# Four side slots for conditioning rows: ten chunks in the mixer seam, ten between the layers

## What is computed

```python
m = (silu(c) @ cond_w + cond_b).reshape(c.shape[0], 9, 1, D_MODEL)   # D_MODEL = 1024

def pre(i, h):
    return rmsnorm(h, norm_pre[i]) * (1.0 + m[:, 3 * i + 1]) + m[:, 3 * i]

def post(i, h, y, rw):
    return h + rw * m[:, 3 * i + 2] * rmsnorm(y, norm_post[i])

x = post(0, x, swiglu(pre(0, x), ffn_w_in[0], ffn_w_out[0]), 0.5)
x = post(1, x, mixer(pre(1, x)), 1.0)
x = post(2, x, swiglu(pre(2, x), ffn_w_in[1], ffn_w_out[1]), 0.5)
```

## Time and profile before

| | us |
|---|---|
| median of 3 runs | 1402.75 |
| lowest, highest | 1401.98, 1404.49 |
| the profiled execution | 1407.09 |
| its span, first to last instruction | 1405.1 |
| PE busy in it | 1340.8 |
| DVE busy | 810.6 |
| ACT busy | 587.0 |
| POOL busy | 50.5 |

### The profile page before, as it was taken

How to read it: one execution, slowest core, us unless ns; L and a number is a source line. 1 busy time by engine, 2 the same in 40 slices (tenths; PEclk the granted TensorE clock), 3 DMA queues, 4 the chain that set the end, 5 groups by cost and what they waited for, 6 DMA issues and landing times.

```text
span 1405.1 us, 34485 instructions
## 1 busy us (share of the span) xinstructions
PE 1340.8 (95%) x13990; PEld 1277.4 (91%) x13990; DVE 810.6 (58%) x1200; ACT 587.0 (42%) x965; POOL 50.5 (4%) x131
## 2 busy tenths in 40 slices
PE   6999999899989899999989999998998998999997
PEld 4999999899976899999989999998997787999997
DVE  2554453567894655554475555446789657555444
ACT  2533333543564643333463333345236555333442
POOL 4000000100020000000000000001001000000000
PEclk9999999999999999999999999999999998999998
DMA  9978789689989895577588557976997993565552
GB/s 331 273 231 253 209 272 294 185 259 325 293 275 324 251 308 150 157 218 208 164 259 253 150 160 225 318 202 208 324 327 223 319 324 94 152 177 152 145 163 84
DMA packets 423816, 324.49 MB, mean 231 GB/s; under 512 B 15559, under 2 KB 351719, under 8 KB 423696
## 3 DMA queue, kind: packets, MB, share of 16 engines
q1 hardware_dynamic: 421124, 317.03, 74.2%
q0 software_dynamic: 2272, 5.61, 1.3%
q10 hardware_dynamic: 300, 0.13, 0.0%
HBM read 317.93 MB, written 4.78 MB: 230 GB/s over the span
## 4 chain that ended last, share of the span: by engine, by line
PE 83%; DVE 6%; DMA 3%; SPq 3%; ACT 2%; DVEq 1%; issue 1%; ACTq 0%
PE PS L573 23%; PE PS L574 22%; PE PS L575 22%; PE PS L597 4%; PE PS L618 2%; PE PS L825 1%; PE PS L619 1%; PE PS L620 1%; SPq L466 1%; PE PS L871 1%; DMA direct<-in_cache_sb_v 1%; DVE w_lo L1610 1%; DMA raw<-in_ffn_w_in 1%; SPq L445 1%; ACT Y L1288 1%
## 5 line engine op out<-in xcount | busy, mean ns | idle before, releaser
L1610 DVE TENSOR_TENSOR w_lo<-raw,w_hi 128x1024 fp32r<-128x1024 f32 (+1 forms) x368 | 392.6, 1106 | 458.9 <-ACT w_hi L1230 458.7
L1230 ACT ACTIVATE w_hi<-raw 128x1024 fp32r<-128x1024 f32 (+1 forms) x368 | 336.9, 960 | 674.5 <-PE PS L575 601.6
L573 PE MATMUL PS<-a_hi,w_hi 128*128 128x288 f32 x1760 | 524.5, 298 | 0.6 <-issue 0.6
L574 PE MATMUL PS<-a_lo,w_hi 128*128 128x288 f32 x1760 | 519.7, 295 | 0.0
L575 PE MATMUL PS<-a_hi,w_lo 128*128 128x288 f32 x1760 | 518.1, 294 | 0.0
L573 PEld LDWEIGHTS PS<-a_hi,w_hi 128*128 128x128 f32 x1760 | 330.1, 188 | 3.8 <-issue 3.5
L575 PEld LDWEIGHTS PS<-a_hi,w_lo 128*128 128x128 f32 x1760 | 331.6, 188 | 0.0
L574 PEld LDWEIGHTS PS<-a_lo,w_hi 128*128 128x128 f32 x1760 | 330.6, 188 | 0.9 <-issue 0.7
L574 PE MATMUL PS<-h_lo,w_hi 128*128 128x288 f32 x704 | 209.1, 297 | 0.0
L573 PE MATMUL PS<-h_hi,w_hi 128*128 128x288 f32 x704 | 208.7, 296 | 0.0
L575 PE MATMUL PS<-h_hi,w_lo 128*128 128x288 f32 x704 | 208.5, 296 | 0.0
(11 more groups left out here) (320 smaller groups left out, 1119.8 us busy)
## 6 DMA issues: line engine op xcount, KB each, us to landing
raw<-in_ffn_w_in SPq DMA_DIRECT2D x176, 512.0 KB, 5.1
direct<-in_cond_w SPq DMA_DIRECT2D x288, 256.0 KB, 5.2
direct<-in_cache_sb_k SPq DMA_DIRECT2D x128, 256.0 KB, 4.3
direct<-in_cache_sb_v SPq DMA_DIRECT2D x128, 256.0 KB, 4.3
raw<-in_ffn_w_out SPq DMA_DIRECT2D x64, 384.0 KB, 3.7
raw<-in_mix_w_in SPq DMA_DIRECT2D x48, 512.0 KB, 7.3
raw<-in_ffn_w_out SPq DMA_DIRECT2D x64, 320.0 KB, 4.3
raw<-in_mix_w_out SPq DMA_DIRECT2D x16, 512.0 KB, 7.7
```

The costliest lines, as they stand in the source:

```text
L573: pe.matmul(out, whi, hi, start=begins and i == 0, stop=False)
L574: pe.matmul(out, whi, lo, start=False, stop=False)
L1230: act.activation(w_hi[:, s, at_:at_ + n], raw[:, s, at_:at_ + n], ACT.Copy)\
L1610: tt(w_lo[:, s, at_:at_ + n], raw[:, s, at_:at_ + n], w_hi[:, s, at_:at_ + n], ALU.subtract).then_inc(lo_done.sem, 1)
```

## The change

Four tiles of 8 KB per partition, `side0` to `side3`, take four more chunks (slots of 1 MB). `side0` and `side1` lie in the memory of `a_hi` and `a_lo`, which is idle during the output products. `side2` and `side3` lie where the mixer has `lrw_hi`, `lrw_lo`, `lr_raw` and some of what follows them. They serve group 2 of each layer and group 1 of layer 1. Twelve chunks of such a group are now eight in `direct` and four in `side`.

- **PE.** Behind the output chunks of the first FFN only two chunks are left of six (behind output chunk 5). `mixer_seam` has ten. `layer_seam` has ten in place of seven, and the input products of layer 1 two in place of five. The sums of squares of `x` are made pair by pair (`pair_squares`), with a chunk between them.
- **PSUM.** The sums of the three column blocks `c` go to three neighbouring ranges of banks 6 and 7, so that PE need not wait for a copy between them. `copy_wide` takes three at once.
- **SP.** The order of the loads of the rows: four for `direct`, two into `side2` and `side3`, for the first FFN two more for `direct`, and two into `side0` and `side1`, all between the loads of output weights.
- **POOL** waits for the fourth `side` chunk, where it waited for the sums of squares of `y`.
- **ACT** waits for the second `side` chunk before it writes `a_hi`.
- Two semaphores for the spread roots become one (`root_spread`).

```diff
+            def part_chunk(l, i, c, slot):
+                k = direct_in[slot]
+                pe.wait_ge(k.sem, (k.at(l, DP_C[i] // 4 + 1) + c // 2) * 64)
+                if c == 0 and slot % 2 == 0:
+                    pe.wait_ge(cond_copied.sem, cond_copied.at(l, 6 * i - 6))
+                cond_products(direct[:, slot, :], slot, c).then_inc(direct_used.sem, 1)
+
+            def side_chunk(l, i, slot):
+                pe.wait_ge(side_in.sem, side_in.at(l, i - 1) * 64 * NSIDE)
+                cond_products(side[slot][:, :], slot, 1).then_inc(side_used.sem, 1)
...
-                        if s % 3 == 2 and not final:
+                        if s == 2 and n == 0:
+                            for slot in (2, 3):
+                                part_chunk(l, 1, 2, slot)
+                        elif s % 3 == 2 and n == 1 and not final:
                             for c in ((7, 8, 9), (10, 11))[s // 3]:
                                 cond_chunk(l, *cond_in, *divmod(c, 4))
...
-                group(0, True, 4 if n == 0 else 0)
+                group(0, True)
                 if n == 0:
                     group(1, chunks=2)
...
-                filled_seam(l, 0, 1, DP_C[2], 6, 10, 12, l)
+                mixer_seam(l)
...
-                    filled_seam(l, 2, 0, DP_C[1], 0, 4, 7, l + 1)
+                    layer_seam(l)
```

The parts on SP, ACT, DVE and POOL:

```diff
-                        if i * 4 + s < 10:
-                            cond(l, 2, i, s)
+                        if i == 0:
+                            cond_part(lc, x, 0, s)
+                        if i == 1 and s >= 2:
+                            if l + n and s == 2:
+                                sp.wait_ge(ss_out.sem, ss_out.at(l + n, 0) * 32)
+                            cond_side(lc, x, s)
+                        if i == 2 and s < 2 and n == 0:
+                            cond_part(lc, x, 2, s)
+                        if i == 2 and s >= 2:
+                            sp.wait_ge(w_used.sem, w_used.at(l, POS_IN[n] + N_IN))
+                            cond_side(lc, x, s - 2)
...
+                if p < 2:
+                    act.wait_ge(side_used.sem, side_used.at(l, NSIDE * p - NSIDE + 2))
...
+            def copy_wide(l, i):
+                for pair in range(2):
+                    dve.wait_ge(direct_used.sem, direct_used.at(l, DP_C[i] + 4 + 2 * pair + 2))
+                    cp(crow[:, :].rearrange("p (c h x) -> p c h x", h=2, x=P)[:, :, pair, :],
+                       PS[:, 6 + pair, 0:3 * P].rearrange("p (c x) -> p c x", x=P))
+                dve.drain()
+                dve.sem_inc(cond_copied.sem, 6)
...
-                for pair in range(2):
-                    copy_sums(direct_used.at(l, DP_C[2]), 2, pair)
+                copy_wide(l, 2)
...
-                after(ssy_done, l, 1)
+                after(side_used, l, NSIDE)
```

More of the change, by code:

```diff
@@ L232, in decoder_step @@
         assert at[0] <= TOP, at[0] - TOP
+        side = [tile(f"side{j}", [P, 2048], F32, here) for j, here in enumerate(
+            (a_region, a_region + 8192, crow_end, crow_end + 8192))]
+        assert a_region + 16384 <= a_end
         dm = tile("dm", [P, GP, T], F32, y_region)
@@ L526, in _ @@
                 mix_in(0, 1)
-                cond_seam(l, 2, 10, 12)
+                for s in range(2, 4):
+                    cond_part(l, 2, 2, s)
                 mix_in(2, 3)
@@ L552, in _ @@
                         ffn_in(l + 1, 0, s, s)
-                    cond_seam(l + 1, 1, 4, 8)
+                    for s in range(4):
+                        cond_part(l + 1, 1, 2, s)
             for h in range(2):
@@ L753, in filled_seam @@
                     cond_chunk(layer, x, dp, *divmod(n, 4))
-                seam_squares(l, seam)
+                for j in range(KP):
+                    pair_squares(l, seam, j)
                 spread_x(*divmod(3 * l + seam + 1, 3))
@@ L1760, in ffn @@
                         hidden(j, j % 2)
-                        if j % 3 == 2 and not final:
+                        if j == 2 and n == 0:
+                            copy_wide(l, 1)
+                        elif j % 3 == 2 and n == 1 and not final:
                             for c, pair in (((1, 1), (2, 0)), ((2, 1),))[j // 3]:
```

133 lines of the change are left out of this document (83 added, 50 removed).

## The result

| | before | after |
|---|---|---|
| median, us | 1404.13 (6 runs, 1401.98 to 1405.47) | 1391.54 (6 runs, 1389.11 to 1392.85) |
| profiled execution | 1407.09 | 1392.76 |
| its span | 1405.1 | 1391.0 |
| mean granted clock | 0.973 | 0.981 |

The ratio is 0.9911, with a 95% interval of 0.9898 to 0.9924: 12.6 us less.

A forecast was written before the change was run, and what follows sets the result against it. PE, busy 95% of the span, was taken as the bound, with unused PE time in the seams. Terms 8.3 + 3.0 + 0.5 + 0.4 = 12.2 us, off the median 1402.75, gave 1390.5 us, range 1388.7 to 1396.0.

The forecast's parts named there:

- Output products, 8.3: Output products of the first FFN: two pairs of chunks leave in each layer, 2.08 us a pair, 8.3 us gained.
- Input products of layer 1 and first step between the layers, 3.0 + 0.4: Layer 1's input products go from five chunks to two, 3.0 us; between the layers the first step ends 0.4 us earlier.
- The seam takes the chunks up: Seam before the mixer: six chunks between the spreads, three more than before, leave `spread_x` as early or a tenth or two later.
- the tight fit: Seam before the mixer: six chunks and three sums take 7.04 us by printed durations, in a room of 6.99 us.
- The clock, 0.5: Mixer seams: the clock stays at 2.4 GHz, `spread_x` takes 0.46 us and not 0.72, 0.26 us gained in each, 0.5 us.
- a rival of chance: The clock falls all the same in the seams: 8.7 us gained, 1394.0 us, up to 1400; chance 0.22.
- Layer 0's first mixer step, taken as 0, bounds 0 to 1.3: Layer 0's mixer: the first step ends 1.6 us earlier, but later waits may take it back; gain 0 to 1.3, taken as 0.
- The load that was to hold the last chunk up: Behind `spread_x` in layer 0's mixer seam: the last chunk's load arrives at 284.33 both before and after, so it sets that chunk.
- `copy_wide`, 1.0 for two, and POOL: Mixer: two wide copies take 1.0 us (0.5 to 1.4); POOL's last small load lands at 287.9, 6.9 us after issue.
- the wait of 0 to 0.4: Mixer, each layer: PE, ready at 291.8, waits up to 0.4 us for `copy_wide` ending at 292.2; counted as 0.
- 0.7 us to spare: Layer 0's mixer: POOL's last small load lands at 287.9, 0.7 us before ACT wants it, so nothing is late.
- The sum: Whole kernel: 8.3 + 3.0 + 0.5 + 0.4 = 12.2 us, set against the median 1402.75, gives 1390.5 us.

The follow-up runs named there:

- light loads: Changed kernel, but SP's row loads inside the two new kinds of seam carry 32 of 512 columns, so the conditioning is stale: 1390.47 us in one execution.
- the run with one chunk more: Changed kernel with one idle chunk (16 products nobody reads) added between the two spreads of each new seam, ahead of the first sum: 1397.34 us, 0.9951.
- the run with the third seam interleaved: Changed kernel with chunks also put between the sums of squares of x before the second FFN, three in both layers: 1395.06 us, 0.9941.
- the run with the sums last: Changed kernel with the sums of squares of x behind all chunks between the spreads in the new seams, as before the change: 1392.52 us, 0.9919.
- the second run: The changed kernel once more, unchanged, beside the last experiment: 1391.58 us, 0.9914.
- the run with POOL 6.8 us later: Changed kernel with POOL's small loads and clearing held back until the first pair of the mixer's operands is ready: 1390.07 us, 0.9902.
- Idle products for warmth: Idle chunks between sums: in the changed kernel before the second FFN, 1391.16 us, 0.9907; in the kernel before, mixer and layer seams, 1408.07 us, 1.0027.

## Why the prediction was right, and where not

- **Output products, 8.3.** Exact: 4.16 in each layer, and 2.08 a pair when one was put back. This is the mechanism of the prediction, and it is shown both ways.
- **Input products of layer 1 and first step between the layers, 3.0 + 0.4.** Came as 2.86. The 3.0 is right: from the last product of the first step on, the stage takes 126.76 us before and 123.79 after, 2.97 less. The 0.4 was the step that failed. The last product of the first step starts 21.55 us behind the sums of `y` before and 21.66 after. The prediction let `spread_x` and DVE's operands come as before and the three chunks run through. The chunks stopped for 1.10 us, but that is the small part: with light loads and no stop the last product starts at 21.54. The larger part is that `spread_x` comes 10.69 us behind the sums of `y` and not 10.42, and the third pair of operands 18.32 and not 18.00. The delay starts on ACT, ahead of `spread_y`:

```profile
708.89 0.26 ACT L1368 ACTIVATE rstd<-rstd 128x72 f32<-128x72 f32 x1 [0.37 <-issue]
```

  This pause is 0.37 us in all ten profiles with the changed program, and 0.07 before (from the end of the one at 714.81 to 715.21). What ACT waits for there no run shows.
- **The seam takes the chunks up.** Right: in layer 0 10.48 us from the sums of `y` to `spread_x` before and after, in layer 1 10.63 and 10.48. But it was not the tight fit that was counted. From start to start the six chunks leave room for a seventh, as the run with one chunk more shows. What is tight is something the prediction didn't know: where the borders of PE's instruction blocks fall. That the long stops of the mixer seams stand behind `spread_x`, where the first step absorbs them, and not ahead of it, is luck.
- **The clock, 0.5.** It held in the three filled seams in both profiles of the changed kernel. It is not certain: it fell in the run with the third seam interleaved, at the same code, behind a stop of 0.31 us, and in the run with the sums last. The prediction called that a rival of chance without a run that showed it; now there is one. Its price was set too high, as the run with the sums last shows. The Trainium skill, "TensorE: Matmul & The Clock Gate", "What's actually happening", on which the prediction drew for this rival, says that the number of slow matmuls differs from run to run of one kernel. The trace agrees: the two profiles of the changed kernel have a mean granted clock of 0.981 and 0.989.
- **Layer 0's first mixer step, taken as 0, bounds 0 to 1.3.** This was mis-sized. The stage gained 1.16 us in layer 0, 0.9 more than the clock's 0.26, and it was not given back: the mixer's end stands 5.46 us earlier, the turn 5.38. The argument was that the loads hold a faster PE up, as in layer 1, where PE idled 1.4 us. But PE is never idle in 288 to 366, and the 1.4 us were not all a wait for loads. They are two rows of before, and the third is all that is idle in layer 1 after:

```profile
1006.36 0.86 PE L825 MATMUL PS<-direct,qb 128*32 128x128 f32 x24 [0.84 <-DVE direct L1877]
1020.82 0.29 PE L573 MATMUL PS<-a_hi,w_hi 128*128 128x288 f32 x1 [0.56 <-issue]
...
1007.83 0.29 PE L604 MATMUL PS<-a_hi,w_hi 128*128 128x288 f32 x1 [1.26 <-issue]
```

  0.56 of the 1.4 is a stop for instructions, 1.43 us behind the end of a block. The time of the step itself was worked out well: its end at 291.8, less the 4.22 by which the sums of `y` start earlier, is 287.58, and the last product starts at 287.63. The load that was to hold the last chunk up didn't: in the second run, which has no stop there, the first step starts 14.48 us behind the sums of `y`, where 14.75 was counted. In layer 1 the same stage took 0.15 more. DVE pauses there in all ten profiles with the changed program, so that the second pair of operands comes 2.16 us behind the first and not 1.89:

```profile
954.17 0.88 DVE L1806 SCALAR_TENSOR_TENSOR a_lo<-Y,M,a_hi 128x256 fp32r<-128x256 f32 x2 [0.18 <-issue]
```

  Of the 0.35 us that the first pair gains (14.68 to 14.33 behind the sums of `y`) the third keeps 0.07. And the turn has to wait for `copy_wide`, which ends at 959.55 + 1.02 = 960.57, and the turn starts at 960.65; before the change the copies ended at 973.73 and the turn began at 974.13.
- **`copy_wide`, 1.0 for two, and POOL.** Two wide copies take 1.01 us:

```profile
286.88 1.01 DVE L1710 COPY crow<-PS 128x384 f32<-128x384 f32 x2
...
274.90 1.03 POOL L2310 DMA_DIRECT2D lr_raw<-in_mix_w_in  x1 [249.93 <-PE PS L632]
...
sb_col<-in_sb_bias POOLq DMA_DIRECT2D x1, 0.0 KB, 5.0
```

  They end at 287.89, right ahead of the turn at 287.98, so the wait of 0 to 0.4 is there: PE's last product starts at 287.63, and 0.13 later it would be free. POOL began 0.8 us behind the fourth `side` chunk, as counted. The landing took 5.0 us and not the 6.9 of the earlier trace rows, and ACT did not wait. 0.7 us to spare was on the careful side, as the run with POOL 6.8 us later shows: there the DMA engines moved 16 GB/s from 281.6 to 288.5, and a landing takes 2.2 to 3.0 us, where they moved 231 from 274.9 to 282.0 in after.
- **The sum.** Forecast 12.2; the four changed stages gave 12.2, of parts that missed by -0.5, +0.9 and -0.4. That the sum agrees to a tenth is luck; that the chunks which left the full stretches gave 8.32 and 2.97, forecast with 8.3 and 3.0, is not. The measured 12.6 holds these and whatever the unchanged stages add or take in one pair of executions.

**Open:** what ACT and DVE wait for in their pauses of 0.37 and 0.18 us; whether the block of instructions starts late because of the DMA traffic, of which one run speaks; and what decides, at the same code, whether the clock falls.

## What to carry to other kernels

Price a move from start to start in a stretch where the engine is never idle, and look for its new place in a stage where a chain of other engines sets the end: 8.3 and 3.0 us came as 8.32 and 2.97. The effects on the clock were small or chance. Count the gap from start to start as well, since printed durations overlap and make it look full. And when an engine stops with no releaser, look at the landings of its instruction blocks. One chunk more did not overfill the gap, but moved such a stop ahead of the chain that sets the end, and cost three times its own duration. Idle products for warmth gained at most 1.5 us in the one stage where nothing else needed PE, and nothing for the kernel.

## What the runs showed of the hardware

- PE can run out of instructions: it stops inside a run of short independent products with no semaphore, for up to 2.35 us, and goes on 1.25 to 1.53 us after a 16 KB block of the instruction queue has landed. The places lie at fixed counts of products, 128 apart, the length differs from run to run. Long products are not exempt: 288.0 to 366.0 has no stop (78.00 us of 78.00, at 333 GB/s), but in layer 1 PE stops behind product 10373, inside products of 128x288, for 0.22 to 1.26 us in eight profiles (1007.83 in after).
- The granted clock fell at the same code at which it held. In the changed kernel it held with this ahead, and with the third seam interleaved it fell at 280.3 with the second line ahead:

```profile
276.50:279.90 3.40, 2.12 (x61) 1.77 (x65) 2.16 (x5) 2.54 (x7) 3.40 (x5) 1.00 1.07 281
```

```profile
276.90:280.30 3.40, 2.04 (x60) 1.29 (x53) 2.27 (x5) 2.56 (x6) 3.40 (x6) 1.00 1.02 303
```

- A small load from POOL lands in 4.8 to 6.0 us among SP's loads in the changed kernel (3.8 to 6.9 before), and in 2.2 to 3.0 when these have thinned out.
